# DeltaNet stage of a two-layer hybrid model: the first gate block computed behind the second convolution block, and the output projection's weight splits spread over the levels of the inverse

## The chip, the core and the metric

The kernel runs on one core of one Trainium2 chip. A core has five engines that run side by side and wait for one another on semaphores: TensorE (PE, matrix multiplication), VectorE (DVE), ScalarE (ACT), GpSimd (POOL) and SyncE (SP, here the queue that loads weights). The metric is the device time of one execution in microseconds.

## The reference, cut to what matters

Two layers over 256 tokens of width 1024: sliding-window attention with a dense feed-forward, then a gated DeltaNet with a mixture of 8 experts. The change touches only the gated DeltaNet:

```python
def gated_deltanet(h, w_in, conv_w, a_log, dt_bias, o_norm, w_o):
    proj = h @ w_in                       # 1024 x (4*1024 + 16)
    qkv, z, b, a = split(proj)            # 3072, 1024, 8, 8 columns
    qkv = silu(causal_depthwise_conv(qkv, conv_w))   # 4 taps
    q, k, v = heads(qkv)                  # 8 heads of 128
    q, k = l2_normalize(q), l2_normalize(k)
    beta = sigmoid(b); g = -exp(a_log) * softplus(a + dt_bias)
    o = chunked_gated_delta_rule(q, k, v, g, beta)   # needs a triangular inverse
    o = rms_norm(o, o_norm) * silu(z)     # z is the gate
    return o @ w_o
```

All of it is computed in float32.

## The kernel before

A float32 product is made of three TensorE products of float32r halves: every weight block of 128 x 2048 numbers is loaded by SP into one of 6 raw slots (`w_raw`), split by ScalarE into a high part (`split_high`, line 278, `w_high`) and by VectorE into a low part (`split_low`, line 282, `w_low`), each with 3 slots, and then used by TensorE (`mm3`, lines 290 to 292). Block n may be split once block n-3 has been used (semaphore `w_used`), TensorE may use it once its low part is there (`lo_done`), and SP may load block n once block n-6 has been split.

Nothing plans the order at run time: each engine has its own program, written out by hand, and goes through it in order. In the DeltaNet stage the input projection is 8 column blocks of 512, two weight blocks ("halves") each, in the order of `GDN_COLS`: six for q, k and v (`conv(c, half)`), which go through the convolution, and two for the gate z (`gate_piece`). They use weight blocks 0 to 15, the output projection blocks 16 to 19.

A convolution block c goes through this chain: `conv` on TensorE; `first_tap` on ScalarE (line 660); `taps`, 12 instructions on VectorE (line 1672) that read the product from PSUM; `silu` on ScalarE (line 667); `tokens` on TensorE (line 1092), which turns it to rows of tokens; for q and k also `squares` (676), `norms` on GpSimd (461 to 465), `normed` on VectorE (1683), `turn_back` on TensorE (1102) and `turned_back` on ScalarE (683). Beside it the decay is made: once `gate_done` is set, TensorE sums the gates (line 1145), ScalarE copies them (`gcum`, 704, `egc`, 705), GpSimd builds a difference (454) and `gate_rows` (1112), `exponent` (1689) and `decay_exp` (688) finish it. `key_key` (1116) and `lower` (1695, 1697) give the matrix that is inverted, `key_query` (1120) the attention within a chunk.

The inverse goes in levels 1 to 5. In each, TensorE runs `step` (1211) for two halves t of the tokens, VectorE subtracts from the identity (1768), TensorE runs `update` (1224, 1233), ScalarE and VectorE copy the results (756, 765, 1772), and GpSimd masks the matrix for the next level (`masked`, 487) and does a multiplication of its own (500, 502, 504, then 508 with the gate). Pieces of the gate's second block fill TensorE up to level 2. Behind level 2 ScalarE takes the second block of z (`gate_silu(1)`, 744) and splits blocks 16, 17 and 18; VectorE splits 16 and 17 there and 18 behind level 3.

After the inverse come the scan over the two chunks, the output projection, and the experts, which take most of the time.

Of the kernel before, what the change touches and what calls it, by code (L numbers as in the profile page):

```python
# [73 lines left out]
def hybrid_kernel(nc, x, a_norm, a_w_qkv, a_b_qkv, a_sinks, a_w_o, f_norm, f_w_gate, f_w_up, f_w_down,  # L74
# [14 lines left out]
    with ExitStack() as ctx:  # L89
# [130 lines left out]
        GDN_COLS = (2, 3, 0, 1, 4, 5, 6, 7)  # L220
# [308 lines left out]
        def _(act):  # L529
# [111 lines left out]
            def deltanet(n0):  # L641
# [13 lines left out]
                def first_tap(c):  # L655
                    act.wait_ge(w_used, n0 + 2 * c + 2)
                    cb = GDN_COLS[c]
                    for f in range(4):
                        w = 32 + 24 * (TAPS - 1) + 4 * cb + f
                        last = nc.scalar.activation(cv[:, 4 * cb + f, :], PS[:, 2 * (c % 2) + f // 2, T * (f % 2):T * (f % 2) + T],  # L660
                                                    ACT.Copy, scale=cols[:, w:w + 1])
                    last.then_inc(sem("tap0_done"), 1)

                def silu(c):
                    act.wait_ge(sem("taps_done"), c + 1)
                    cb = GDN_COLS[c]
# [22 lines left out]

                split_high(act, n0 + 3)  # L690
# [17 lines left out]
                silu(1)  # L708
                split_high(act, n0 + 8)
                first_tap(2)  # L710
# [4 lines left out]
                split_high(act, n0 + 9)  # L715
                silu(2)
                split_high(act, n0 + 10)
# [4 lines left out]
                split_high(act, n0 + 11)  # L722
                silu(3)
                split_high(act, n0 + 12)
# [16 lines left out]
                def gate_silu(c):  # L741
                    act.wait_ge(w_used, n0 + 14 + 2 * c)
                    for t in range(TT):
                        nc.scalar.activation(z[:, t, c * CH:(c + 1) * CH], PS[:, Z + t, :], ACT.Silu).then_inc(sem("z_done"), 1)
# [160 lines left out]
        def _(pe):  # L905
# [154 lines left out]
            def deltanet(n0):  # L1060
# [3 lines left out]
                def conv(c, half):  # L1064
                    n = n0 + 2 * c + half
                    pe.wait_ge(lo_done, n + 1)
                    if c >= 2 and half == 0:
                        pe.wait_ge(sem("taps_done"), c - 1)
                    wh, wl = high_low(n, 4)
                    for f in range(4):  # L1070
                        for kk in range(4):
# [4 lines left out]
                            last = mm3(PS[:, 2 * (c % 2) + f // 2, T * (f % 2):T * (f % 2) + T], wh[:, kk, col], wl[:, kk, col],  # L1076
# [3 lines left out]
                def tokens(c):  # L1080
                    cb = GDN_COLS[c]
# [6 lines left out]
                    elif c == 5:  # L1088
                        pe.wait_ge(sem("taps_done"), 6)
# [32 lines left out]
                def gate_piece(c, half, t, k0, k1):  # L1122
                    n = n0 + 12 + 2 * c + half
# [18 lines left out]
                conv(1, 1)  # L1142
                pe.wait_ge(sem("gate_done"), 1)
# [32 lines left out]
                pe.wait_ge(sem("taps_done"), 5)  # L1176
                for half in range(2):
                    for t in range(TT):
                        gate_piece(0, half, t, 0, 4)
# [57 lines left out]
                pe.wait_ge(sem("z_done"), 2)  # L1237
# [220 lines left out]
        def _(dve):  # L1458
# [197 lines left out]
            def deltanet(n0):  # L1656
# [7 lines left out]
                def taps(c):  # L1664
                    dve.wait_ge(sem("tap0_done"), c + 1)
                    cb = GDN_COLS[c]
                    for j in range(1, TAPS):
                        for f in range(4):
# [3 lines left out]
                            last = V.scalar_tensor_tensor(out=o, in0=PS[:, 2 * (c % 2) + f // 2, at:at + T - j], scalar=cols[:, w:w + 1],  # L1672
# [51 lines left out]
                split_low(dve, n0 + 7)  # L1724
                exponent(0, B)
                split_low(dve, n0 + 8)
# [6 lines left out]
                split_low(dve, n0 + 9)  # L1733
                split_low(dve, n0 + 10)
                taps(3)
                normed(2)
                split_low(dve, n0 + 11)
                split_low(dve, n0 + 12)
# [25 lines left out]
                for l in range(1, LEVELS):  # L1764
# [8 lines left out]
                    if l == 2:  # L1773
# [270 lines left out]
```

## Time and profile before

| | |
|---|---|
| median of 3 runs | 1637.07 us (1633.76 to 1637.22) |
| the profiled execution's own time | 1634.98 us |
| its span in the profile | 1633.4 us |
| mean granted clock of TensorE | 0.959 of full speed |
| TensorE busy | 1530.7 us (94%) |
| VectorE, ScalarE, GpSimd busy | 1214.0, 993.9, 94.0 us |
| weight loads of this stage | 16 of `in_b_w_in`, 1 MB each, 5.4 us to land |

Read the span first, then the shares. TensorE is busy nearly all the time, but this is an average: the experts' part (from about 663 us) is dense, and the DeltaNet stage (about 387 to 630 us) has waits. What a change of order there is worth is therefore read in the timeline of that stage: which wait of TensorE ends last at which place. "Idle before <- releaser" at the end of a row tells how long the engine had nothing to do before the row's first instruction, and who let it go. Starts and ends of TensorE instructions overlap by a tenth or two of a microsecond, since they are pipelined.

### The profile page before, as it was taken

The page shows a single profiled execution, that of the slowest core. Times are in us where ns is not written, and L with a number is a line of the kernel's source. Part 1 is how long each engine was busy: PE and PEld are TensorE (multiplying, and loading weights), DVE is VectorE, ACT ScalarE, POOL GpSimd, SP SyncE. Part 2 cuts the span into 40 slices and gives each one's busy share as a digit, 9 for nine tenths or more (in the row PEclk, how much of TensorE's full clock was granted, in tenths as well). Part 3 has the DMA queues.
Part 4 walks back from the last instruction along what each step waited for, and adds up shares of the span by engine and source line. Part 5 has one row for each costly group of instructions (what it writes and reads, how often), then busy time and mean ns, then how long its engine had stood idle before and what let it go on. Part 6 is the DMA issues. An engine that isn't in the chain of part 4 may idle for free.

```text
span 1633.4 us, 22310 instructions
## 1 busy us (share of the span) xinstructions
PE 1530.7 (94%) x8225; PEld 1292.4 (79%) x8225; DVE 1214.0 (74%) x983; ACT 993.9 (61%) x931; POOL 94.0 (6%) x104
## 2 busy tenths in 40 slices
PE   5888999998989777899999999999999999999996
PEld 4777888877988676788888888888888888888884
DVE  5744555555576535788888888888888889888887
ACT  4444343434673434577777777777777777777773
POOL 0002000000122401100000000000000000000200
PEclk9789999998899878899999999999999999999998
DMA  9217755553332203699999999999999999999992
GB/s 341 92 39 272 285 187 181 193 191 105 104 129 79 80 1 104 244 377 376 389 380 364 398 375 374 392 377 375 390 367 383 382 381 376 383 380 360 417 409 86
DMA packets 92603, 453.96 MB, mean 278 GB/s; under 512 B 9872, under 2 KB 10256, under 8 KB 49552
## 3 DMA queue, kind: packets, MB, share of 16 engines
q1 hardware_dynamic: 83680, 430.83, 70.0%
q0 software_dynamic: 5616, 20.45, 3.1%
q10 hardware_dynamic: 3264, 2.08, 0.5%
q8 instruction: 31, 0.51, 0.1%
q14 instruction: 12, 0.10, 0.0%
HBM read 437.60 MB, written 15.73 MB: 278 GB/s over the span
## 4 chain that ended last, share of the span: by engine, by line
PE 90%; ACT 4%; DVE 4%; issue 1%; ACTq 1%; POOL 0%; DVEq 0%; POOLq 0%
PE PS L290 27%; PE PS L292 27%; PE PS L291 27%; PE PS L1348 1%; PE PS L917 1%; ACT w_high L278 1%; DVE w_low L282 1%; PE PS L991 1%; PE PS L1233 1%; ACT xs L562 1%; PE PS L967 1%; PE PS L1280 0%; PE PS L1224 0%; PE PS L980 0%; ACTq L549 0%
## 5 line engine op out<-in xcount | busy, mean ns | idle before, releaser
L282 DVE TENSOR_TENSOR w_low<-w_raw,w_high 128x2048 fp32r<-128x2048 f32 x408 | 936.1, 2297 | 238.5 <-ACT w_high L278 238.0
L278 ACT ACTIVATE w_high<-w_raw 128x2048 fp32r<-128x2048 f32 x408 | 781.3, 1918 | 361.1 <-PE PS L292 359.0
L290 PE MATMUL PS<-w_high,x_high 128*128 128x512 f32 x1264 | 501.5, 397 | 5.9 <-DVE x_low L1866 4.5
L292 PE MATMUL PS<-w_high,x_low 128*128 128x512 f32 x1264 | 494.1, 391 | 0.0
L291 PE MATMUL PS<-w_low,x_high 128*128 128x512 f32 x1264 | 493.6, 391 | 0.0
L290 PEld LDWEIGHTS PS<-w_high,x_high 128*128 128x128 f32 x1264 | 238.4, 189 | 56.1 <-DVE x_low L1866 4.6
L292 PEld LDWEIGHTS PS<-w_high,x_low 128*128 128x128 f32 x1264 | 238.1, 188 | 50.8
L291 PEld LDWEIGHTS PS<-w_low,x_high 128*128 128x128 f32 x1264 | 238.5, 189 | 47.4
L290 PE MATMUL PS<-w_high,m_act_high 128*128 128x512 f32 x448 | 175.0, 391 | 1.6 <-DVE m_act_low L1929 1.6
L292 PE MATMUL PS<-w_high,m_act_low 128*128 128x512 f32 x448 | 174.4, 389 | 0.0
L291 PE MATMUL PS<-w_low,m_act_high 128*128 128x512 f32 x448 | 174.4, 389 | 0.0
L290 PEld LDWEIGHTS PS<-w_high,m_act_high 128*128 128x128 f32 x448 | 84.1, 188 | 19.0 <-DVE m_act_low L1929 1.8
L292 PEld LDWEIGHTS PS<-w_high,m_act_low 128*128 128x128 f32 x448 | 84.1, 188 | 17.5
L291 PEld LDWEIGHTS PS<-w_low,m_act_high 128*128 128x128 f32 x448 | 84.1, 188 | 17.2
L833 ACT ACTIVATE m_act_high<-PS 128x512 fp32r<-128x512 f32 x56 | 33.6, 600 | 70.1 <-PE PS L1348 70.1
L290 PE MATMUL PS<-x_high,w_high 128*128 128x256 f32 x192 | 57.2, 298 | 0.0
L291 PE MATMUL PS<-x_low,w_high 128*128 128x256 f32 x192 | 56.1, 292 | 0.0
L292 PE MATMUL PS<-x_high,w_low 128*128 128x256 f32 x192 | 56.0, 292 | 0.0
L917 PE MATMUL PS<-cst,xs 128*128 128x128 f32 x96 | 21.9, 422 | 32.6 <-DVE xs L1481 25.2
L917 PEld LDWEIGHTS PS<-cst,xs 128*128 128x128 f32 x96 | 19.6, 225 | 34.5 <-DVE xs L1481 26.7
L1495 DVE TENSOR_TENSOR h<-PS,h 128x512 f32<-128x512 f32 x36 | 22.6, 685 | 30.4 <-PE PS L292 30.4
L290 PE MATMUL PS<-w_high,f_act_high 128*128 128x512 f32 x112 | 44.4, 397 | 0.7 <-DVE f_act_low L1623 0.7
(272 smaller groups left out, 1282.8 us busy)
## 6 DMA issues: line engine op xcount, KB each, us to landing
w_raw<-in_m_w_blocks SPq DMA_DIRECT2D x336, 1024.0 KB, 7.0
w_raw<-in_b_w_in SPq DMA_DIRECT2D x16, 1024.0 KB, 5.4
w_raw<-in_f_w_gate SPq DMA_DIRECT2D x14, 1024.0 KB, 5.0
w_raw<-in_f_w_up SPq DMA_DIRECT2D x14, 1024.0 KB, 5.0
w_raw<-in_f_w_down SPq DMA_DIRECT2D x14, 1024.0 KB, 4.8
w_raw<-in_a_w_qkv SPq DMA_DIRECT2D x6, 1024.0 KB, 13.1
x_slots_dram<-zeros POOLq DMA_DIRECT2D x12, 512.0 KB, 7.5
w_raw<-in_a_w_o SPq DMA_DIRECT2D x4, 1024.0 KB, 6.9
```

What stands on the lines that cost most here:

```text
L278: nc.scalar.activation(WH[:, n % SPLIT, :], W[:, n % RAW, :], ACT.Copy).then_inc(hi_done, 1)
L282: nc.vector.tensor_tensor(WL[:, n % SPLIT, :], W[:, n % RAW, :], WH[:, n % SPLIT, :].bitcast(f32), ALU.subtract).then_inc(lo_done, 1)
L290: nc.tensor.matmul(o, sH, mH, start=first, stop=False)
L291: nc.tensor.matmul(o, sH, mL, start=False, stop=False)
L292: return nc.tensor.matmul(o, sL, mH, start=False, stop=last)
L562: nc.scalar.activation(xs[:, t], h[:, t], ACT.Square, accum_out=ss[:, n, t:t + 1]).then_inc(ss_done, 1)
L833: nc.scalar.activation(maH[:], PS[:, 4, :].rearrange("p (f q) -> p f q", f=4), ACT.Copy)\
L917: last = nc.tensor.transpose(PS[:, 4 + b, 256 * kk + 128 * t:256 * kk + 128 * t + 128], src[:, t, 128 * k:128 * k + 128], ident)
L967: last = nc.tensor.matmul(PS[:, 2 * (a % 2) + hh % 2, col:col + nk], qkT[r, hd // 2, 128 * t:128 * t + 128], qkT[r, 8 + g, 0:nk], start=Tr ...
L991: last = nc.tensor.matmul(PS[:, 6 + a % 2, 64 * hh:64 * hh + 64], probT[:, a % 2, hh * (t + 1) + kt, :], qkv[:, kt, 1280 + 64 * g:1280 + 6 ...
L1233: last = nc.tensor.matmul(PS[halves(s), A + s, HALF * hh:HALF * hh + HALF], Zt[halves(s), t, hh, :], X[halves(s), t, hh, :], start=True, s ...
L1495: return V.tensor_tensor(h[:, t, cb * CH:(cb + 1) * CH], PS[:, bank, :], h[:, t, cb * CH:(cb + 1) * CH], ALU.add)
```

## The change

The weight blocks are taken in another order: the gate's first column block (6) becomes the third of the eight. TensorE computes it (48 products of 512 columns) directly behind `conv(1)`, ahead of the wait for `gate_done`, where it used to run behind `key_key(1)`, after the last convolution block. ScalarE's `gate_silu(0)` moves from behind `silu(5)` to behind `silu(1)`. `CONV_AT` and `GATE_AT` give the place of each block among the eight, `CONV_BANK` the PSUM banks of each convolution block: blocks 2 and 3 change places, so that `conv(2)` waits for `taps(1)` and `conv(3)` for the gate's SiLU. The splits of blocks 4 to 15 move with the blocks. Of the output projection's blocks, 16 is now split behind `v_evict(4)` and `taps(5)`, 17 behind level 1, and 18 behind level 3 on both engines; none behind level 2.

```diff
-        GDN_COLS = (2, 3, 0, 1, 4, 5, 6, 7)
+        GDN_COLS = (2, 3, 6, 0, 1, 4, 5, 7)
+        CONV_AT = (0, 1, 3, 4, 5, 6)
+        GATE_AT = (2, 7)
+        CONV_BANK = (0, 2, 2, 0, 2, 0)
...
                 def first_tap(c):
-                    act.wait_ge(w_used, n0 + 2 * c + 2)
-                    cb = GDN_COLS[c]
+                    act.wait_ge(w_used, n0 + 2 * CONV_AT[c] + 2)
+                    cb = GDN_COLS[CONV_AT[c]]
...
+                def gate_silu(c):
+                    act.wait_ge(w_used, n0 + 2 * GATE_AT[c] + 2)
+                    for t in range(TT):
+                        nc.scalar.activation(z[:, t, c * CH:(c + 1) * CH], PS[:, Z + t, :], ACT.Silu).then_inc(sem("z_done"), 1)
...
                 squares(0)
                 split_high(act, n0 + 7)
                 silu(1)
+                gate_silu(0)
                 split_high(act, n0 + 8)
+                split_high(act, n0 + 9)
+                split_high(act, n0 + 10)
                 first_tap(2)
...
-                split_high(act, n0 + 13)
+                split_high(act, n0 + 15)
                 silu(4)
-                split_high(act, n0 + 14)
                 first_tap(5)
...
                 v_evict(4)
-                split_high(act, n0 + 15)
+                split_high(act, n0 + 16)
                 silu(5)
-                gate_silu(0)
                 turned_back(3)
                 v_evict(5)
...
+                    if l == 1:
+                        split_high(act, n0 + 17)
                     if l == 2:
                         gate_silu(1)
-                        split_high(act, n0 + 16)
-                        split_high(act, n0 + 17)
+                    if l == 3:
                         split_high(act, n0 + 18)
...
                 def conv(c, half):
-                    n = n0 + 2 * c + half
+                    n = n0 + 2 * CONV_AT[c] + half
                     pe.wait_ge(lo_done, n + 1)
-                    if c >= 2 and half == 0:
-                        pe.wait_ge(sem("taps_done"), c - 1)
+                    if half == 0 and c == 3:
+                        pe.wait_ge(sem("z_done"), 2)
+                    elif half == 0 and c >= 2:
+                        pe.wait_ge(sem("taps_done"), (2, 0, 3, 4)[c - 2])
...
                 conv(1, 0)
                 conv(1, 1)
+                pe.wait_ge(sem("taps_done"), 1)
+                for half in range(2):
+                    for t in range(TT):
+                        gate_piece(0, half, t, 0, 4)
                 pe.wait_ge(sem("gate_done"), 1)
...
                 key_key(1)
-                pe.wait_ge(sem("taps_done"), 5)
-                for half in range(2):
-                    for t in range(TT):
-                        gate_piece(0, half, t, 0, 4)
                 pe.wait_ge(sem("u_read"), 2)
                 turn_back(3)
                 tokens(5)
...
-                pe.wait_ge(sem("z_done"), 2)
+                pe.wait_ge(sem("taps_done"), 6)
                 gate_piece(1, 0, 0, 0, 4)
...
                 normed(0)
                 split_low(dve, n0 + 7)
+                split_low(dve, n0 + 8)
                 exponent(0, B)
-                split_low(dve, n0 + 8)
+                split_low(dve, n0 + 9)
+                split_low(dve, n0 + 10)
                 taps(2)
...
-                split_low(dve, n0 + 13)
+                split_low(dve, n0 + 15)
                 lower(0)
-                split_low(dve, n0 + 14)
                 lower(1)
                 taps(5)
-                split_low(dve, n0 + 15)
+                split_low(dve, n0 + 16)
...
-                    if l == 2:
-                        split_low(dve, n0 + 16)
+                    if l == 1:
                         split_low(dve, n0 + 17)
                     if l == 3:
                         split_low(dve, n0 + 18)
```

What is left out: the definitions of `silu`, `taps` and `tokens`, which take their column block and banks from the new tables, `gate_silu`'s old place, the numbers of the splits between `taps(2)` and `taps(4)` (each higher by 2), and `tokens(5)`, which waits for `taps(4)` instead of `taps(5)`.

TensorE's order behind `conv(1)`, before: the last products of `conv(1)` (128x256), the sums of the gates (gate,cst), `tokens(0)` (cst,cv), then `conv(2)`.

```order
L290 MATMUL PS<-x_high,w_high 128x256
L291 MATMUL PS<-x_low,w_high 128x256
L292 MATMUL PS<-x_high,w_low 128x256
L1145 MATMUL PS<-gate,cst 128x16 x2
L1092 MATMUL PS<-cst,cv 128x128 x8
L290 MATMUL PS<-x_high,w_high 128x256
```

The same place after the change: the last products of the gate block (128x512), the sums, `tokens(0)`, `conv(2)`.

```order
L293 MATMUL PS<-w_high,x_high 128x512
L294 MATMUL PS<-w_low,x_high 128x512
L295 MATMUL PS<-w_high,x_low 128x512
L1156 MATMUL PS<-gate,cst 128x16 x2
L1099 MATMUL PS<-cst,cv 128x128 x8
L293 MATMUL PS<-x_high,w_high 128x256
```

The sums of the gates now stand behind the 48 products of the gate block instead of directly behind `conv(1)`.

VectorE's order in the inverse, before, from the first level: `step` is the subtraction, invT the copy of a level's result, w_low a split.

```order
L1768 TENSOR_TENSOR step<-cst,PS 64x512 x4
L1772 COPY invT<-PS 64x512 x2
L1768 TENSOR_TENSOR step<-cst,PS 64x512 x4
L1772 COPY invT<-PS 64x512 x2
L282 TENSOR_TENSOR w_low<-w_raw,w_high 128x2048 x2
L1768 TENSOR_TENSOR step<-cst,PS 64x512 x4
L1772 COPY invT<-PS 64x512 x2
L282 TENSOR_TENSOR w_low<-w_raw,w_high 128x2048
L1768 TENSOR_TENSOR step<-cst,PS 64x512 x4
```

The same place after the change.

```order
L1776 TENSOR_TENSOR step<-cst,PS 64x512 x4
L1780 COPY invT<-PS 64x512 x2
L285 TENSOR_TENSOR w_low<-w_raw,w_high 128x2048
L1776 TENSOR_TENSOR step<-cst,PS 64x512 x4
L1780 COPY invT<-PS 64x512 x2
L1776 TENSOR_TENSOR step<-cst,PS 64x512 x4
L1780 COPY invT<-PS 64x512 x2
L285 TENSOR_TENSOR w_low<-w_raw,w_high 128x2048
L1776 TENSOR_TENSOR step<-cst,PS 64x512 x4
```

The two splits between levels 2 and 3 are gone; one stands between levels 1 and 2, the other of them ahead of the inverse.

## Rows read from the trace of the kernel before

**Rows 1.** The timeline, TensorE behind conv(1): start us, us, engine line op

```profile
425.15 0.62 PE L1145 MATMUL PS<-gate,cst 128*128 128x16 f32 x4 [1.64 <-DVE beta L1716]
426.86 1.81 PE L1092 MATMUL PS<-cst,cv 128*128 128x128 f32 x8 [1.09 <-ACT cv L667]
437.81 0.36 PE L290 MATMUL PS<-x_high,w_high 128*128 128x256 f32 x1
443.65 1.03 PE L1092 MATMUL PS<-cst,cv 128*128 128x128 f32 x8
```

**Rows 2.** The timeline, ScalarE, GpSimd and VectorE ahead of the second half of conv(2)

```profile
429.94 0.20 ACT L704 ACTIVATE gcum<-PS 128x16 f32<-128x16 f32 x1
431.70 3.75 POOL L454 TENSOR_TENSOR decay<-cst,gcum 128x1024 f32<-128x1024 f32 x2 [4.52 <-ACT egc L705]
437.60 1.29 DVE L1683 TENSOR_TENSOR tok<-PS,rq 128x512 f32<-128x512 f32 x2 [1.65 <-POOL rq L462]
438.81 2.28 DVE L282 TENSOR_TENSOR w_low<-w_raw,w_high 128x2048 fp32r<-128x2048 f32 x1
```

**Rows 3.** The timeline, TensorE, from the end of conv(5) to the gate's second block

```profile
493.92 1.03 PE L1092 MATMUL PS<-cst,cv 128*128 128x128 f32 x8
496.50 0.47 PE L290 MATMUL PS<-w_high,x_high 128*128 128x512 f32 x1
507.49 1.03 PE L1102 MATMUL PS<-cst,tok 128*128 128x128 f32 x8
509.75 3.84 PE L1120 MATMUL PS<-cv 128*128 128x128 f32 x32 [0.34 <-ACT cv L683]
513.34 0.47 PE L290 MATMUL PS<-w_high,x_high 128*128 128x512 f32 x1
```

**Rows 4.** The timeline, VectorE and ScalarE, the last convolution block

```profile
498.33 1.38 DVE L1695 TENSOR_TENSOR u_diag<-PS,decay 64x512 f32<-64x512 f32 x2
500.36 5.00 DVE L1672 SCALAR_TENSOR_TENSOR cv<-PS,cols,cv 128x255 f32<-128x255 f32 x12
505.39 1.06 ACT L667 ACTIVATE cv<-cv 128x1024 f32<-128x1024 f32 x1 [1.17 <-DVE cv L1672]
```

**Rows 5.** The timeline, TensorE, levels 2 to 4 of the inverse

```profile
531.41 2.03 PE L1211 MATMUL PS<-invT,u_level 64*64 64x64 f32 x64
536.34 1.15 PE L1224 MATMUL PS<-step,inv 64*64 64x64 f32 x32
540.70 2.03 PE L1211 MATMUL PS<-invT,u_level 64*64 64x64 f32 x64
552.06 1.97 PE L1224 MATMUL PS<-step,inv 64*64 64x64 f32 x32 [9.33 <-DVE step L1768]
558.01 2.03 PE L1211 MATMUL PS<-invT,u_level 64*64 64x64 f32 x64
561.73 1.15 PE L1224 MATMUL PS<-step,inv 64*64 64x64 f32 x32 [0.67 <-DVE step L1768]
```

**Rows 6.** The timeline, ScalarE and VectorE behind level 2 of the inverse

```profile
542.13 1.08 ACT L744 ACTIVATE xs<-PS 128x512 f32<-128x512 f32 x2
543.10 5.51 ACT L278 ACTIVATE w_high<-w_raw 128x2048 fp32r<-128x2048 f32 x3
550.62 2.80 DVE L1768 TENSOR_TENSOR step<-cst,PS 64x512 f32<-64x512 f32 x4
```

**Rows 7.** The timeline, GpSimd beside the levels, and the VectorE split at its third row

```profile
535.10 1.89 POOL L502 TENSOR_TENSOR tok<-tok,egc 128x1024 f32<-128x1024 f32 x1
559.20 2.20 POOL L487 TENSOR_TENSOR u_level<-u_diag,cst 128x512 f32<-128x512 f32 x1 [12.96 <-PE PS L1211]
557.97 2.29 DVE L282 TENSOR_TENSOR w_low<-w_raw,w_high 128x2048 fp32r<-128x2048 f32 x1
```

**Rows 8.** The windows: TensorE's granted clock is the third number from the right

```profile
425.00:430.00 5.00, 3.75 (x20) 3.66 (x21) 1.46 (x2) 4.99 (x8) 2.02 (x2) 0.71 0.37 142
```

**Rows 9.** The timeline, TensorE behind a longer wait, at tokens(3)

```profile
478.12 1.85 PE L1102 MATMUL PS<-cst,tok 128*128 128x128 f32 x8 [3.56 <-ACT cv L683]
```

More of the change, by code:

```diff
@@ L655, in first_tap @@
                 def first_tap(c):
[L656 to L657 removed]
+                    act.wait_ge(w_used, n0 + 2 * CONV_AT[c] + 2)
+                    cb = GDN_COLS[CONV_AT[c]]
                     for f in range(4):
                         w = 32 + 24 * (TAPS - 1) + 4 * cb + f
[L660 removed]
+                        last = nc.scalar.activation(cv[:, 4 * cb + f, :], PS[:, CONV_BANK[c] + f // 2, T * (f % 2):T * (f % 2) + T],
                                                     ACT.Copy, scale=cols[:, w:w + 1])
@@ L714, in deltanet @@
                 squares(1)
-                split_high(act, n0 + 9)
+                split_high(act, n0 + 11)
                 silu(2)
-                split_high(act, n0 + 10)
+                split_high(act, n0 + 12)
                 first_tap(3)
@@ L1075, in conv @@
                             col = slice(128 * f, 128 * f + 128)
-                            last = mm3(PS[:, 2 * (c % 2) + f // 2, T * (f % 2):T * (f % 2) + T], wh[:, kk, col], wl[:, kk, col],
+                            last = mm3(PS[:, CONV_BANK[c] + f // 2, T * (f % 2):T * (f % 2) + T], wh[:, kk, col], wl[:, kk, col],
                                        xH[:, k, :], xL[:, k, :], k == 0 and f % 2 == 0, k == KD - 1 and f % 2 == 1)
@@ L1122, in gate_piece @@
                 def gate_piece(c, half, t, k0, k1):
-                    n = n0 + 12 + 2 * c + half
+                    n = n0 + 2 * GATE_AT[c] + half
                     pe.wait_ge(lo_done, n + 1)
@@ L1175, in deltanet @@
                 key_key(1)
-                pe.wait_ge(sem("taps_done"), 5)
-                for half in range(2):
-                    for t in range(TT):
-                        gate_piece(0, half, t, 0, 4)
                 pe.wait_ge(sem("u_read"), 2)
@@ L1671, in taps @@
                             at = T * (f % 2)
-                            last = V.scalar_tensor_tensor(out=o, in0=PS[:, 2 * (c % 2) + f // 2, at:at + T - j], scalar=cols[:, w:w + 1],
+                            last = V.scalar_tensor_tensor(out=o, in0=PS[:, CONV_BANK[c] + f // 2, at:at + T - j], scalar=cols[:, w:w + 1],
                                                           in1=o, op0=ALU.mult, op1=ALU.add)
@@ L1732, in deltanet @@
                 normed(1)
-                split_low(dve, n0 + 9)
-                split_low(dve, n0 + 10)
+                split_low(dve, n0 + 11)
+                split_low(dve, n0 + 12)
                 taps(3)
                 normed(2)
-                split_low(dve, n0 + 11)
-                split_low(dve, n0 + 12)
+                split_low(dve, n0 + 13)
+                split_low(dve, n0 + 14)
                 taps(4)
                 normed(3)
-                split_low(dve, n0 + 13)
+                split_low(dve, n0 + 15)
                 lower(0)
-                split_low(dve, n0 + 14)
                 lower(1)
                 taps(5)
-                split_low(dve, n0 + 15)
+                split_low(dve, n0 + 16)
                 for t in range(TT):
```

15 lines of the change are left out of this document (6 added, 9 removed).

## The prediction

> **What bounds the kernel now.** I read the page first: TensorE is busy 94% of the span. Then I read the windows over the DeltaNet stage, to see where it is not, and then the timeline of TensorE there, and at each of its waits the timeline of the engine that ends it. Three places matter, since the change touches them.
>
> Behind `conv(1)` TensorE waits 1.64 us for the gates and, after a few tiny products, 1.09 us for `silu(0)` [rows 1]. The clock granted in that stretch is 0.71 on average [rows 8], so for part of it the engine ran at 1.2 instead of 2.4 GHz; eight transposes take 1.81 us where they take 1.03 us later [rows 1]. So this is a real hole, a few microseconds deep.
>
> From the end of `conv(5)` on TensorE has hardly a wait: `tokens(4)` and `key_key(1)` from 493.92 to 496.50, the gate block to 507.49, then `turn_back(3)` and `tokens(5)`, and `key_query` from 509.75 to 513.34 [rows 3]. In that time VectorE and ScalarE finish the last convolution block [rows 4]. The gate block (10.99 us) is their cover.
>
> In the inverse TensorE stands still for 9.33 us behind level 2 [rows 5], since ScalarE first does the gate's SiLU and three splits (5.51 us) and VectorE two splits before its subtractions [rows 6].
>
> **The change, part by part.** The work itself is unchanged in number and size: the same 48 products, the same splits, the same SiLU. No load is larger, and blocks are requested when an older one has been split, two places ahead as before. I give the loads nothing: the blocks that the change hurries (4 to 7) were asked for long before. What changes is who waits where.
>
> *Front.* TensorE leaves `conv(1)` at about 423.4 (the row at 425.15 less its wait, and a little overlap) and goes on with the gate block, 10.99 us, to 434.35. Its two weight blocks are split by then. The sums of the gates follow, 0.62 us [rows 1], done at 434.97. Only now may ScalarE copy them. From that copy to the end of a split on VectorE the chain takes 429.94 to 441.09, that is 11.15 us: copy and table load and exponential on ScalarE, two differences on GpSimd (3.75 us), the norms there, two multiplications on VectorE, the split [rows 2]. Before, that split was for a block needed much later. Now it is `split_low(7)`, and the second half of `conv(2)` needs it. So that half starts at 434.97 + 11.15 + 0.05 = 446.17, where it started at 437.81 [rows 1]: +8.4 us, with a gate block of 10.99 us done in between. The hole is smaller by 2.6 us, and not closed. TensorE reaches this wait at about 443.6, from the end of `taps(1)` at 435.9 with half a block (437.81 to 443.65, 5.84 us) and the 16 `gate_rows` of 1.8 us behind it (an estimate from twice the eight transposes), so it stands for 2.5 us. From there to the end of `conv(5)` every engine does the same as before, 8.4 us later; splits two blocks further on are as far ahead of their use as before.
>
> *Tail.* Behind `key_key(1)` the gate block is gone. `lower(1)` starts when `key_key(1)` is done, 2.58 us after the end of `conv(5)` plus 0.3 for the last product to end. Then come `lower(1)`, 2.03 (498.33 to 500.36), `taps(5)`, 5.03, `silu(5)`, 1.06 [rows 4], `tokens(5)`, 0.9, and `key_query`, 3.59 (509.75 to 513.34) [rows 3]. With 0.05 for the handover that is 2.58 + 0.3 + 2.03 + 5.03 + 1.06 + 0.05 + 0.9 + 3.59 = 15.5 us, against 513.34 - 493.92 = 19.4 us before. So removing 10.99 us of work wins 3.9 us here. TensorE now waits about 2.1 us for `lower(1)` (its u_read) and 5 us for `silu(5)`. `turn_back(3)` between them is off the path.
>
> *Inverse.* Behind level 1 ScalarE has its turn 1.4 us after the next step has started (542.13 less 540.70), splits block 17 in 1.84 us (a third of 5.51), and VectorE splits it in 2.29 us and makes half of its subtractions in 1.4 us [rows 5 to 7]. With handovers, `update` starts 7.05 us after `step`. In level 2 it started 4.93 us after it (531.41 to 536.34), behind a gate piece: +2.1 us. Level 3 loses its wait of 9.33 us: `step` to `update` takes 1.19 (559.20 less 558.01) + 1.40 = 2.6 us instead of 11.36, and `update` to the next `step` 4.36 (536.34 to 540.70) instead of 5.95 [rows 5 to 7]: -10.4 us. In level 4 the split of block 18 by both engines again gives 7.05 us instead of 3.72: +3.3 us. Sum: 2.12 - 10.35 + 3.33 = -4.9 us.
>
> GpSimd makes this worse. At 559.20 its masking of 512 columns took 2.20 us, more than 1024 columns at 535.10 (1.89 us), while VectorE's split ran until 560.26 [rows 7]. So one of these two engines holds the other off. Behind level 1 the split now meets GpSimd's masking and its `egc` multiplication, and behind level 3 the masking and the multiplication by `o_w`, twice 1024 columns. If the split only waits for a masking that has begun, each costs 0.4 us more. If it must also wait for the multiplication, it is 1.9 us and 3.8 us (twice 1.89) more. I take 0.4 at both places and half of 1.9 at the first: +1.8 us. So the inverse wins 3.1 us, with bounds of a gain of 4.9 and a loss of 1.6 us (all three).
>
> The Trainium skill, "GPSIMD Engine Reference", section "Specifications", says that GpSimd shares its SBUF interfaces with VectorE, and that contention is with instructions in a two-port mode or with two SBUF inputs. By it the splits are hit and `taps`, which read PSUM, are not; the row at 559.20 agrees. Without that rule and row the sum would be 1.8 us lower.
>
> *The clock.* After a wait of 3.56 us eight transposes took 1.85 us [rows 9], as after the 1.64 and 1.09 us at the front [rows 1]; in level 3 the slow stretch cost 5.95 - 4.36 = 1.6 us. So I price a fall at 1.6 us. At the tail there are 7 us of waits: 2.0 (1.6 to 3.4). In level 4 the wait is near 5 us: 1.2. The 2.5 us at `conv(2)` and the 2.5 us or more in level 2 may or may not bring a fall: 0.7 and 0.6, each between 0 and 1.6. The fall behind `tokens(3)` may not come again: -0.5 (-1.6 to 0). Sum +4.0 us.
>
> The Trainium skill, "TensorE: Matmul & The Clock Gate", section "Why this matters for your kernels", warns only of idle gaps above about 3 us. By it the two waits of 2.5 us would cost no clock, and the sum would be 1.3 us lower; rows 1, where two shorter waits brought a fall, speak against it.
>
> *Sum.* 8.4 - 3.9 - 3.1 + 4.0 = +5.4 us. Behind the inverse all is as before, and the experts start later by what the stage is longer. The profiled execution took 1634.98 us (span 1633.4), so the sum gives 1640.4. That execution lies 2.1 us below the median of the runs (1637.07) and 1.2 above the fastest; I go about a quarter of the way to the median and forecast 1641.0 us.
>
> **The rivals.** *A tie.* VectorE gets ahead of GpSimd at both places and the two doubtful falls of the clock don't come: 8.4 - 3.9 - 4.1 + 1.6 + 0.5 - 0.5 = +2.0 us, 1637.0 to 1639. For it speaks that VectorE's split at 557.97 was not held off [rows 7]. Against it, GpSimd was the second to come there.
>
> *Faster.* The tail's cover is not needed, and the hole at the front closes. This decides if the chain of `lower(1)`, `taps(5)` and `silu(5)` takes at most 1 us more than TensorE's other work: then the tail wins the whole 10.99 us, and the stage moves by 8.4 - 11 - 4.1 + 1 = -5.7 us, to 1629. If the split of block 7 also came in time, it would be -8, 1627. For it speaks the wait of 9.33 us, which goes for certain. Against it, the rows of the last block add up to 8.1 us without any wait inside, and VectorE can't begin sooner, as its order puts `lower(1)` ahead of `taps(5)`.
>
> *Much slower.* GpSimd's multiplications go first at both places and the clock falls at every wait: 8.4 - 3.9 + 1.6 + 7 = +13, 1648. It needs three coincidences.
>
> *The change does nothing.* The new block is not split in time and TensorE waits at its new place for what it waited for before. The splits of blocks 4 and 5 were not late for `conv(2)` before, so this has little to stand on; 1637.
>
> **How the numbers follow.** Less than 0.2%, 3.3 us, can't be told from no change. The forecast (+3.3 to +9) has 0.50, much slower 0.12, the tie 0.24, nothing 0.05, faster 0.09. So slower 0.62, same 0.29, faster 0.09. The range leaves out most of "faster" and the end of "much slower": 1635.5 to 1647.
>
> **What would show it.** Right: a TensorE wait near 2.5 us ahead of the second half of `conv(2)`, released by VectorE's split; waits near 2 and 5 us between `key_key(1)` and `tokens(5)`; no wait of 9 us in the inverse, but one of 2 to 4 us in level 2 and of 4 us or more in level 4, both released by the subtraction; splits there longer than 2.3 us where GpSimd runs. Wrong: `conv(2)` without a wait, `tokens(5)` within 1 us of `turn_back(3)`, or an experts' part whose length differs from before.

## The result, and the profile after

| | before | after |
|---|---|---|
| median | 1634.38 us (7 runs, 1633.39 to 1640.55) | 1646.54 us (7 runs, 1640.34 to 1649.28) |
| profiled execution: span, mean granted clock | 1633.4 us, 0.959 | 1647.7 us, 0.951 |

The ratio is 1.0064, with a 95% interval of 1.0044 to 1.0084: the change makes the kernel slower, by about 10 us (1634.4 x 0.0064). The two medians are 12.2 us apart; the ratio comes from all the runs. The forecast was 1641.0 us, +5.4. Three of the seven runs lie above 1647, the upper end of the stated range.

The timeline of TensorE behind `conv(1)` in the changed kernel (start us, us, engine, line, operation; the wait before it and its releaser in brackets):

```profile
436.88 0.51 PE L1156 MATMUL PS<-gate,cst 128*128 128x16 f32 x4
448.62 0.38 PE L293 MATMUL PS<-x_high,w_high 128*128 128x256 f32 x1 [2.21 <-DVE w_low L285]
455.96 1.03 PE L1099 MATMUL PS<-cst,cv 128*128 128x128 f32 x8
```

The waits of 1.64 and 1.09 us [rows 1] are gone, and a new one of 2.21 us stands where the prediction put it, released by VectorE's split. The half block behind it takes 7.34 us (448.62 to 455.96) instead of 5.84: the clock fell. The chain that sets it, answering to rows 2, on ScalarE, GpSimd and VectorE:

```profile
437.42 0.18 ACT L712 ACTIVATE gcum<-PS 128x16 f32<-128x16 f32 x1 [4.74 <-PE PS L1156]
...
439.17 3.75 POOL L457 TENSOR_TENSOR decay<-cst,gcum 128x1024 f32<-128x1024 f32 x2 [9.37 <-ACT egc L713]
...
445.08 1.29 DVE L1690 TENSOR_TENSOR tok<-PS,rq 128x512 f32<-128x512 f32 x2 [5.71 <-POOL rq L465]
446.28 4.48 DVE L285 TENSOR_TENSOR w_low<-w_raw,w_high 128x2048 fp32r<-128x2048 f32 x2
```

The first of the two splits in the last row is block 7. From 437.42 to 448.57, its end, are 11.15 us, as before.

The tail, answering to rows 3, on TensorE:

```profile
506.20 1.03 PE L1099 MATMUL PS<-cst,cv 128*128 128x128 f32 x8
507.07 1.95 PE L1123 MATMUL PS<-cv 128*128 128x128 f32 x16
511.29 1.72 PE L1109 MATMUL PS<-cst,tok 128*128 128x128 f32 x8 [2.27 <-DVE u_cross L1704]
517.30 1.97 PE L1099 MATMUL PS<-cst,cv 128*128 128x128 f32 x8 [4.30 <-ACT cv L670]
519.06 5.06 PE L1127 MATMUL PS<-cv 128*128 128x128 f32 x32
523.88 0.47 PE L293 MATMUL PS<-w_high,x_high 128*128 128x512 f32 x1
```

Two waits have taken the gate block's place, 2.27 us for `lower(1)` and 4.30 us for `silu(5)`, and the two groups of eight transposes and `key_query` behind them run partly at the half clock (5.06 instead of 3.84 us).

The inverse, answering to rows 5, on TensorE:

```profile
541.97 2.03 PE L1218 MATMUL PS<-invT,u_level 64*64 64x64 f32 x64
...
549.31 1.97 PE L1231 MATMUL PS<-step,inv 64*64 64x64 f32 x32 [2.33 <-DVE step L1776]
...
555.12 2.03 PE L1218 MATMUL PS<-invT,u_level 64*64 64x64 f32 x64
...
562.07 2.03 PE L1218 MATMUL PS<-invT,u_level 64*64 64x64 f32 x64
...
569.39 1.81 PE L1231 MATMUL PS<-step,inv 64*64 64x64 f32 x32 [4.26 <-DVE step L1776]
```

Level 3 (555.12 to 562.07) takes 6.95 us instead of 17.3; the wait of 9.33 us has become one of 2.33 in level 2 and one of 4.26 in level 4. Beside them, VectorE and GpSimd, answering to rows 7:

```profile
545.35 2.50 DVE L285 TENSOR_TENSOR w_low<-w_raw,w_high 128x2048 fp32r<-128x2048 f32 x1 [3.98 <-ACT w_high L281]
...
565.45 2.47 DVE L285 TENSOR_TENSOR w_low<-w_raw,w_high 128x2048 fp32r<-128x2048 f32 x1 [3.98 <-ACT w_high L281]
```

```profile
545.66 3.94 POOL L505 TENSOR_TENSOR tok<-tok,egc 128x1024 f32<-128x1024 f32 x1
...
565.72 6.58 POOL L511 TENSOR_TENSOR xs<-xs,o_w 128x2048 f32<-128x2048 f32 x1
```

The split loses 0.2 us, and it is GpSimd that is held off: 3.94 instead of 1.89 us. This costs nobody anything.

Behind the inverse the code is the same in both kernels, and yet it is longer. The windows from the first product of the output projection to the experts' first transposes, and from there to the choice of tokens (busy times of PE, PEld, DVE, ACT, POOL; third from the right the granted clock), before:

```profile
607.99:635.25 27.26, 22.05 (x99) 17.93 (x97) 10.30 (x13) 8.79 (x10) 1.98 (x4) 1.00 0.33 106
635.25:651.87 16.62, 13.08 (x74) 12.87 (x75) 11.69 (x30) 8.42 (x12) 4.67 (x2) 0.60 0.22 80
```

and after:

```profile
618.10:646.61 28.51, 23.30 (x99) 18.87 (x97) 10.30 (x13) 8.79 (x10) 1.98 (x4) 0.92 0.30 102
646.61:666.15 19.54, 16.01 (x75) 15.82 (x75) 11.59 (x30) 8.44 (x12) 4.68 (x2) 0.50 0.17 67
```

In the second window the clock is at 1.2 GHz from end to end, where before it was at 2.4 GHz for a part; that is 2.92 us, and 1.25 us in the first. Nothing waits longer for another engine. Below, the *short form* is a profile in which projection and router together take 46.7 to 47.3 us, the *long form* one in which they take 51.0 to 51.4 us; no profile lies between.

This table cuts the profile at fixed places of TensorE's timeline. *Front*: the stage's first transposes to the second half of `conv(2)`; *middle*: to the end of `conv(5)`; *tail*: to the gate's second block; *inverse*: to the last transposes of k and q; *scan*: to the transposes ahead of the projection; *projection*: from those to the experts' first transposes; *router*: from those to the choice. All in us; the runs further down are in it too. The experts take 969.5 to 970.2 us in every one.

| kernel | front | middle | tail | inverse | scan | projection | router |
|---|---|---|---|---|---|---|---|
| before | 50.33 | 56.11 | 19.42 | 62.20 | 29.12 | 30.59 | 16.62 |
| before, 2nd profile | 50.46 | 56.09 | 19.42 | 62.31 | 29.12 | 30.63 | 16.59 |
| after | 58.56 | 57.58 | 17.68 | 60.75 | 30.15 | 31.83 | 19.54 |
| after, 2nd profile | 58.70 | 57.20 | 18.00 | 60.44 | 30.35 | 30.47 | 16.69 |
| after, 3rd profile | 58.51 | 57.56 | 17.70 | 60.70 | 30.15 | 31.86 | 19.56 |
| splits only | 50.34 | 56.12 | 19.45 | 60.57 | 30.62 | 30.60 | 16.55 |
| gate only | 58.61 | 57.13 | 17.96 | 61.85 | 29.10 | 30.35 | 16.77 |
| after, front mended | 56.05 | 56.04 | 17.94 | 60.59 | 30.24 | 30.42 | 16.72 |
| after, tail mended | 58.57 | 57.60 | 15.79 | 59.31 | 30.14 | 31.80 | 19.55 |
| before, splits in the scan | 50.32 | 56.14 | 19.44 | 51.13 | 30.23 | 30.42 | 16.75 |
| after, all three mends | 56.19 | 56.01 | 16.17 | 51.11 | 29.22 | 31.49 | 19.55 |
| splits in the scan, front closed | 44.72 | 57.41 | 19.42 | 51.10 | 29.22 | 31.52 | 19.54 |
| the same, with filler | 44.61 | 57.45 | 19.44 | 51.12 | 30.70 | 29.51 | 17.76 |
| after, with filler | 58.66 | 57.13 | 17.98 | 60.43 | 30.34 | 30.46 | 16.27 |

### The profile page after: what moved, and what is told of

The parts are those of the page before. It is cut to its first block, busy times and chain, and to the rows that moved or that the text cites. A ratio compares the mean times of both kernels' runs of the same rounds, so it can differ in the third digit from the quotient of the medians.

```text
span 1647.7 us, 22310 instructions
## 1 busy us (share of the span) xinstructions
PE 1542.2 (94%) x8225; PEld 1301.9 (79%) x8225; DVE 1213.1 (74%) x983; ACT 994.1 (60%) x931; POOL 97.3 (6%) x104
## 4 chain that ended last, share of the span: by engine, by line
PE 91%; ACT 4%; DVE 3%; POOL 1%; ACTq 1%; issue 1%; POOLq 0%; DVEq 0%
PE PS L293 27%; PE PS L295 27%; PE PS L294 27%; PE PS L1355 1%; PE PS L922 1%; ACT w_high L281 1%; PE PS L996 1%; PE PS L1240 1%; ACT xs L565 1%; PE PS L972 1%; PE PS L985 0%; PE PS L1287 0%; ACTq L552 0%; DVE w_low L285 0%; PE PS L1231 0%
## 5 line engine op out<-in xcount | busy, mean ns | idle before, releaser
L295 PEld LDWEIGHTS PS<-w_high,x_low 128*128 128x128 f32 x1264 | 238.6, 189 | 51.1
```

Source lines behind the costliest of these rows:

```text
L295: return nc.tensor.matmul(o, sL, mH, start=False, stop=last)
```

## The experiments

Theory A: the loss is the sum of the waits and of the clock they bring, as predicted: the gate block had been the cover of the last convolution block. Theory B, formed on the table's last columns: much of it is the clock in code behind the inverse. All timed runs are against the kernel before on the same chip.

**Only the splits moved.** The kernel before, with:

```diff
+                split_high(act, n0 + 16)          # behind v_evict(5)
...
+                    if l == 1:
+                        split_high(act, n0 + 17)
                     if l == 2:
                         gate_silu(1)
-                        split_high(act, n0 + 16)
-                        split_high(act, n0 + 17)
-                        split_high(act, n0 + 18)
+                    if l == 3:
+                        split_high(act, n0 + 18)
```

and the same on VectorE (16 behind the attention products, 17 behind level 1; 18 stays behind level 3).

> The kernel before, with only the output projection's splits moved: block 16 behind the last copies ahead of the inverse, 17 behind level 1, 18 behind level 3 on both engines. The gate block stays where it was. By the theory of the waits, the inverse alone wins what it won in the changed kernel: level 3 about -10.4 us, level 2 about +2.4 and level 4 about +3.6 us of wait, and up to two falls of the clock at 1.45 us each: -1.5 to -4.5 us against the kernel before. The rival, that the splits inside the levels cost as much as they save, expects a tie or slower.

Measured: 1634.27 against 1634.49 us, ratio 0.9997 (0.9988 to 1.0007). A tie; the expected gain of 1.5 us is just inside the interval, 4.5 are not. On TensorE the profile has three waits for the subtractions instead of the one of 9.33 us:

```profile
539.44 1.22 PE L1226 MATMUL PS<-step,inv 64*64 64x64 f32 x32 [2.33 <-DVE step L1771]
547.35 1.15 PE L1226 MATMUL PS<-step,inv 64*64 64x64 f32 x32 [0.55 <-DVE step L1771]
559.03 1.97 PE L1226 MATMUL PS<-step,inv 64*64 64x64 f32 x32 [4.26 <-DVE step L1771]
```

In the table the inverse wins 1.6 us and the scan gives back 1.5 at a granted clock of 0.72 instead of 0.76. So the forecast for the inverse alone was met at its lower end, that for the kernel was not: here this half of the change is worth nothing.

**Only the gate block moved.** The changed kernel with the splits of 16, 17 and 18 back behind level 2 (18's low part behind level 3):

```diff
-                split_high(act, n0 + 16)          # behind v_evict(4), ahead of silu(5)
...
-                    if l == 1:
-                        split_high(act, n0 + 17)
                     if l == 2:
                         gate_silu(1)
+                        split_high(act, n0 + 16)
+                        split_high(act, n0 + 17)
+                        split_high(act, n0 + 18)
-                    if l == 3:
-                        split_high(act, n0 + 18)
```

> The changed kernel with the output projection's splits of blocks 16 and 17 put back behind level 2 (and 18's high part with them): only the gate block is moved. By the theory of the waits this part loses 8.2 us at the front and 1.5 us to the clock in conv(2), wins 1.7 us at the tail, and the inverse is as before: about +8 us against the kernel before. The rival, that most of the loss is the clock in the stages behind the inverse, expects +3 us or less here if the phase of those stages is not hit, and the same +10 as the changed kernel if any shift brings it.

Measured: 1643.11 us, ratio 1.0051 (1.0033 to 1.0070), or +8.3 us, as theory A had it. Its profile shows the short form behind the inverse (30.35 and 16.77 us), and is still 9.7 us longer than before: front +8.3, middle +1.0, tail -1.5, the later stretches -0.5 together, and 2.5 us of it ahead of the stage, in code that is the same. The rival that expected 3 us or less is out; the same +10 as the changed kernel lies within the interval (+5.4 to +11.4), but not by way of the long form, which this profile doesn't have. The loss up to the end of the inverse comes with the gate block's move.

**The front mended.** The changed kernel with:

```diff
                 first_tap(1)
+                split_high(act, n0 + 7)
                 act.wait_ge(sem("gcum_ps"), 1)
...
                 squares(0)
-                split_high(act, n0 + 7)
...
                 taps(1)
+                split_low(dve, n0 + 7)
...
                 normed(0)
-                split_low(dve, n0 + 7)
```

> The changed kernel with the split of block 7 moved ahead of the decay chain on ScalarE and VectorE (behind first_tap(1) and taps(1)). By the theory of the waits TensorE's wait of 2.2 us at the second half of conv(2) goes, and with it the fall of the clock of 1.5 us: -2.5 to -4 us against the changed kernel. If the wait there is not on this split, nothing changes.

Measured: 1637.87 us, ratio 1.0021 (1.0007 to 1.0034), against 1.0064 for the changed kernel. The wait is gone; TensorE goes from `gate_rows` straight on:

```profile
443.02 1.95 PE L1119 MATMUL PS<-cst,gate_wide 128*128 128x128 f32 x16
```

```profile
444.72 0.36 PE L293 MATMUL PS<-x_high,w_high 128*128 128x256 f32 x1
```

In the table front and middle are 4.0 us shorter than in the first profile after (2.5 and 1.5). That is the forecast's upper end. The ratios differ by more, 0.0043 or about 7 us. In the two profiles the rest is in projection and router, which are in the short form here (by 4.2 us); against the second profile after, which has the short form too, front and middle are 3.8 us shorter. What made up the 7 us in the other runs no profile shows.

**The tail mended.** The changed kernel with:

```diff
-                lower(1)
                 taps(5)
+                lower(1)
```

> The changed kernel with taps(5) ahead of lower(1) on VectorE. taps(5) can start when first_tap(5) is done, 3.2 us earlier; turn_back(3) then waits for lower(1) behind it. By the theory of the waits key_query starts about 2 us earlier than in the changed kernel: -1 to -2.5 us. If the tail is not bound by this chain of VectorE, no change.

Measured: 1644.10 us, ratio 1.0046 (1.0027 to 1.0065). The interval overlaps that of the changed kernel, so the time alone doesn't settle it; the table has the tail 1.9 us shorter, as expected (and the inverse 1.4, which was not), with one wait of 6.07 us in place of two:

```profile
513.86 1.97 PE L1109 MATMUL PS<-cst,tok 128*128 128x128 f32 x8 [6.07 <-DVE u_cross L1704]
```

**The splits in the scan.** The kernel before, with block 16 split ahead of the inverse and:

```diff
+                split_high(act, n0 + 17)          # ahead of the levels
...
+                split_high(act, n0 + 18)          # behind the copies "tg"
...
                         last.then_inc(sem("zt_done"), 1)
+                    if l == 1:
+                        split_low(dve, n0 + 17)
...
+                split_low(dve, n0 + 18)           # behind the cross terms
```

and no split behind levels 2 and 3. Of the three blocks only VectorE's split of 17 is still inside the levels, behind the subtractions of level 1.

> The kernel before, with the output projection's splits where both engines wait anyway: block 16 ahead of the inverse, 17 on ScalarE ahead of level 1 and on VectorE behind the subtractions of level 1, 18 in the scan (behind the copies tg on ScalarE and behind the cross terms on VectorE). By the theory of the waits the three levels have none of the splits' waits: level 3 -10.4 us, level 4 -0.5, and nothing is given back: -9 to -11 us less what the clock takes in the scan (1 to 1.5): about -9 us against the kernel before. The rival, that the clock gives back whatever the inverse wins (as it did when the splits were only spread), expects -3 us or less.

Measured: 1626.13 us against 1635.19, ratio 0.9952 (0.9939 to 0.9965): -7.8 us (the medians are 9.1 apart). The expected 9 are within the interval, the rival's 3 are not. On TensorE level 3 is 6.94 us (541.47 to 548.41) and level 4 has no wait behind the transposes at 550.38:

```profile
541.47 2.03 PE L1211 MATMUL PS<-invT,u_level 64*64 64x64 f32 x64
544.05 1.15 PE L1224 MATMUL PS<-step,inv 64*64 64x64 f32 x32 [0.55 <-DVE step L1769]
...
548.41 2.03 PE L1211 MATMUL PS<-invT,u_level 64*64 64x64 f32 x64
550.38 1.09 PE L1250 MATMUL PS<-cst,tok 128*128 128x128 f32 x8
551.40 1.15 PE L1224 MATMUL PS<-step,inv 64*64 64x64 f32 x32
```

**The changed kernel with all three mends.**

> The changed kernel with three mends at once: block 7's split ahead of the decay chain, taps(5) ahead of lower(1), and the output projection's splits placed as in the run with the splits in the scan. If the place of the gate block costs only what its two new waits cost, this is within 2 us of the kernel before with those splits. If the cover at the tail is worth more than the hole at the front, as the sum of the waits has it (front mended -10.99 + 5.7 + hole, tail 7 us of waits less 2), it is 1 to 4 us slower than that kernel.

Measured: 1628.28 us, ratio 0.9963 (0.9951 to 0.9975). The median is 2.2 us above the unmoved kernel with the same splits (1626.13), but the intervals overlap (0.9939 to 0.9965 there), and its profile has the long form behind the inverse. Up to the end of the inverse the table has 179.5 us against 177.0, so 2.5 us for the move; the scan, with the same code, is 1.0 us shorter. The moved block is then no gain; that it is a loss rests on the profiles, not on the times, and neither of the two expectations (within 2 us, or 1 to 4 us slower) is ruled out.

**The front closed without moving the gate block.** The kernel with the splits in the scan, and on ScalarE:

```diff
                 first_tap(0)
-                split_high(act, n0 + 5)
                 act.wait_ge(sem("gate_in"), 1)
...
                 silu(0)
+                split_high(act, n0 + 5)
                 split_high(act, n0 + 6)
```

on VectorE the same for the gates and `split_low` of block 5, and the difference `kdec` ahead of `taps(1)`.

> The kernel before with the splits in the scan, and the hole at the front closed without moving the gate block: ScalarE makes the gates' exponentials and silu(0) ahead of the split of block 5, while it waits for TensorE, VectorE the same, and the decay's difference ahead of taps(1). By the theory of the waits TensorE no longer waits behind conv(1), and the second half of conv(2) starts 4 to 5.4 us earlier: -4 to -5.5 us against the kernel with the splits in the scan. The rival, that another wait (the decay chain ahead of gate_rows) takes the place, expects -1 us or less.

Measured: 1622.52 us, ratio 0.9925 (0.9912 to 0.9937), or 3.6 us less between the medians than with the splits in the scan alone (1626.13 on the same chip; the intervals don't overlap), and 4.4 by the ratios, where 4 to 5.5 were expected. The front is 5.6 us shorter; the middle, 1.3 us longer, takes part of it back. The profiled execution is the slowest of the five (1628.81; the others 1620.89 to 1623.79): it has the long form, and it enters the stage at 392.85 where the kernel with the splits in the scan does at 388.18. TensorE has no wait left behind `conv(1)`:

```profile
428.84 0.52 PE L1145 MATMUL PS<-gate,cst 128*128 128x16 f32 x4
429.21 1.07 PE L1092 MATMUL PS<-cst,cv 128*128 128x128 f32 x8
```

**Idle products in a wait.** The changed kernel with:

```diff
+                for _ in range(40):
+                    nc.tensor.matmul(PS[:, 7, 0:T], xH[:, 0, 0:128], xH[:, 1, :], start=True, stop=True)
                 turn("moe", xs, xs_done, 2 * (norm_no["moe"] + 1))
```

> The changed kernel with 40 more products of 256 columns on TensorE, whose results nothing reads, directly behind the output projection, in its wait of 5.2 us for the experts' norm. It tests the clock: in the changed kernel's profile the half clock lasts from the projection through the router. If the 2.9 us that the router takes longer there are the clock that the wait brings, the router's stretch is as short as before or shorter (16.6 us or less from its transposes to the choice) and the kernel 1 to 3 us faster than the changed one. If the clock falls there for other reasons, the time is the same within 1 us or longer.

Measured: 1644.38 us, ratio 1.0059 (1.0045 to 1.0073), not to be told from the changed kernel; the gain of 1 to 3 us that was expected if the wait makes the form is not seen. Its router takes 16.27 us, but its projection, ahead of the filler, is already in the short form. So this run doesn't settle what makes the form.

**The changed kernel again**, unaltered, twice, and the kernel before once.

> The changed kernel once more, unaltered, for its spread and a second profile. The profiles so far fall in two groups in the code that the change doesn't touch: projection and router take 47.1 to 47.4 us or 51.0 to 51.4 us. If that is chance of the clock and not of the change, this has both groups in its times, a lower end near 1640 and an upper near 1649, and the ratio is again between 1.004 and 1.008. If the changed kernel is always in the long group, none of its profiles shows the short one.

> The changed kernel, unaltered, for a third profile. From its first transposes to the end of the inverse 194.6 us as in the first, within the clock's falls (1.5 us each); projection and router in either group.

> The kernel before, unaltered, for a second profile. By chance of the clock it may show the long group in projection and router (51 us); if the group belongs to the change, it shows the short one (47.2 us) again. Either way the stage up to the end of the inverse takes 188.1 us from its first transposes.

Measured: 1643.57 us (1640.34 to 1648.18), ratio 1.0062 (1.0045 to 1.0080); the third time, a single run, 1647.43; the kernel before, a single run, 1636.40. Up to the end of the inverse the third profile after has 194.5 us and the second before 188.3, as expected (194.6 and 188.1). The third after has the long form, the second before the short one. The windows of the second profile after, for the same two stretches:

```profile
615.77:643.03 27.26, 22.05 (x99) 17.92 (x98) 10.33 (x13) 8.87 (x11) 1.99 (x4) 1.00 0.32 105
643.03:659.72 16.69, 13.15 (x75) 12.93 (x75) 11.76 (x30) 8.35 (x12) 4.68 (x2) 0.60 0.24 81
```

So the same program takes these 4.1 us in one execution and not in another. The long form doesn't belong to the change alone: three other kernels show it as well. But the times of the changed kernel spread over 9 us (1640.3 to 1649.3 in 14 runs), and those of the kernel before mostly over 5 (1631.5 to 1636.5 in 26 runs; the highest of all is 1640.55). The one profile of the change in the short form has a span 7.4 us above the first of before (1640.8 against 1633.4), those in the long form 12.4 and 14.3 us.

The mean granted clock of each execution is on record too. The changed kernel's seven slowest runs (1646.5 to 1649.3 us) are at 0.951 to 0.953, where its two profiles in the long form are; its other seven (1640.3 to 1645.6) are at 0.955 to 0.961, with the one in the short form. Of the kernel before none of the 48 runs beside the experiments is below 0.959, and its two profiles, both in the short form, are at 0.959 and 0.961. This speaks for the long form being more frequent with the change. It doesn't show it, since the mean is that of the whole execution.

**With idle products in the best kernel.** The kernel with the front closed, with 45 such products ahead of the projection's transposes and 40 ahead of the experts'.

> The kernel before with the splits in the scan and the front closed, and with idle products on TensorE in the two waits ahead of the projection's and the experts' transposes (45 and 40 of 256 columns, results unread). If the clock that these waits bring is what makes projection and router long or short, both are in the short group, and the time is 1 to 4 us below the same kernel without them (1622.5), with less spread. The rival expects no change, or up to 1 us more where a filler ends behind what it waits for.

Measured: 1620.61 us (4 runs, 1618.74 to 1620.92), ratio 0.9912 (0.9898 to 0.9927). It is the fastest of all, about 14 us below the kernel before. Its median is 1.9 us below the same kernel without the filler, as expected, but the intervals overlap (0.9912 to 0.9937 there), and the two ran on different chips. In the profile projection and router take 47.3 us instead of 51.1, and the scan, which holds the first filler, 1.5 us more. The windows:

```profile
592.71:619.93 27.22, 26.79 (x137) 22.84 (x137) 10.50 (x14) 8.66 (x10) 1.99 (x4) 1.00 0.32 109
619.93:637.69 17.76, 13.09 (x74) 12.65 (x74) 13.31 (x30) 8.12 (x12) 6.72 (x2) 0.63 0.19 71
```

But the profile without the filler was the slowest of its five runs, and one profile in the short form may be chance. A gain of the filler is not shown.

## Why the prediction was right, and where its size was off

**The direction and the mechanism.** With the clock's falls put where they were expected, the sum has four parts. *Front* +8.4 us: measured +8.2 (58.56 - 50.33), with the wait released as said, and gone when the split was put elsewhere. *Tail* -3.9 and +2.0 for the clock, -1.9: measured -1.7, and two waits of 2.27 and 4.30 us where 2.1 and 5 were forecast. *Inverse* -3.1 and +1.8 for the clock, -1.3: measured -1.5. *Clock in conv(2)* and behind the wait of 3.56 us of rows 9 (it is at `turn_back(2)`, behind `tokens(3)`), +0.7 and -0.5: measured +1.5, as the first fall came in full and the second again. Up to the end of the inverse this is +6.5 us against a sum of +5.4.

**Two terms that were mis-sized, with a sum that came out by luck.** In the inverse I charged 1.8 us for the interface that VectorE and GpSimd share. The splits took 0.2 us longer each; GpSimd carried the rest, off the path. Without the clock the levels so won 4.3 us, where 3.1 were forecast. What made up for it was the clock, 1.45 us in each of the two levels (the level from 549.31 to 555.12 takes 5.81 us, and 4.36 undisturbed) where I had taken 1.2 and 0.6.

**The step that failed** is "Behind the inverse all is as before". The code is, the clock is not: the scan takes 1.0 us more, and projection and router 4.2 us more in the profiled execution. Of the 14.3 us between the spans, 6.5 are the terms of the sum, 5.2 this, and 2.6 were there before the stage began (390.06 against 387.48), in code that is the same. These 2.6 us are chance: the other two profiles after begin the stage at 387.87 and 388.63, the second before at 388.71. The second profile after, without the long form, is at +7.4 us: 6.3 up to the end of the inverse, 1.2 in the scan. So about 7.5 us of the loss are in a profile of either form, and the long form adds 4.1 to 4.3 where it comes. By the granted clocks above it came in about half of the runs, and that would put the median at 1646.5 rather than 1641; this last step is argued, not shown. The forecast also had some luck with its base: it started from 1634.98 and a median of 1637.07 in three runs, and the kernel before has a median of 1634.38 in seven. So a change of 10 to 12 us, twice the one in the sum, came out only 5.5 us above the forecast, and 0.5 us inside the range.

**The rivals.** "Faster" fell on its own condition: the last block's chain is 6.6 us longer than TensorE's other work (the two waits together), not 1. Of what "A tie" needed, VectorE did get ahead of GpSimd at both places, but the two doubtful falls of the clock came in full. "Does nothing" is out, since the waits moved as the order said. "Much slower" rested on GpSimd going first, which it did not; its 1648 was reached in three of the seven runs all the same, and the profiled one of these got there by another road, the clock behind the inverse.

What stays open: what decides between the short and the long form of projection and router, and whether the change makes the long one more frequent, for which the granted clocks speak, or the executions only fell so. The long form is not bound to the moved gate block: the kernel with the front closed, which leaves the block in its place, has it too.

## What to carry to other kernels

Before moving a block of work out of a place, ask what runs on the other engines beside it: 11 us of products that covered a chain of 8 us on VectorE and ScalarE were worth only 1.7 us when they left, the clock's fall included. Closing a hole with work from elsewhere also pushes back what stood behind the hole, here the first link of a chain of 11 us that fed the next weights; it was cheaper to start the late chain earlier, by putting it ahead of a split that waits for TensorE anyway (-5.6 us at the front, -3.6 between the medians). And work that is needed only some 60 us later should leave the waits of a latency-bound loop: spread over the levels the splits won nothing; ahead of the inverse, behind a level's subtractions and in the scan they won 7.8 us.

## What the runs showed of the hardware

- Of two elementwise instructions with both inputs in SBUF, one on VectorE and one on GpSimd, the later waited for nearly all of the earlier here. Above, the split runs from 545.35 to 547.85; the multiplication on GpSimd, begun at 545.66, ends at 549.60. Had it stood still to 547.85 and then taken its 1.89 us, it would end at 549.74. The other way round, in the kernel before behind `conv(2)`, on VectorE and on GpSimd:

```profile
469.54 2.89 DVE L282 TENSOR_TENSOR w_low<-w_raw,w_high 128x2048 fp32r<-128x2048 f32 x1
```

```profile
468.38 1.90 POOL L470 TENSOR_TENSOR decay<-decay,beta 128x1024 f32<-128x1024 f32 x1
```

  GpSimd ends at 470.28; the split would end at 470.28 + 2.29 = 472.57 and ends at 472.43. The Trainium skill ("SBUF — State Buffer", section "SBUF: two separate sides") says that of a VectorE instruction with two SBUF inputs and a GpSimd instruction that reads SBUF, whichever starts first has the shared pair of ports for the whole instruction, and the other fully blocks. Both pairs here agree with this within 0.14 us. The split that came first took 2.50 us all the same, where 2.29 is usual.
- A wait that is cut in two can cost more clock than one long wait. One wait of 9.33 us brought the half clock once in the inverse (5.95 instead of 4.36 us); waits of 2.33 and 4.26 us brought it twice (5.81 and 5.78 us).
- Behind a wait of 2.21 us the clock fell to 1.2 GHz for a time (48 products took 7.34 instead of 5.84 us); behind one of 1.38 us, at 479.17 in the changed kernel, it did not. The length of the wait doesn't decide alone: behind the same wait of 2.3 us at the end of the inverse the eight transposes took 1.09 us in the kernel before (575.54) and 1.97 in the changed one (584.63).
- The same program shows the router at a granted clock of 0.60 in one execution and 0.50 in the next, 16.7 or 19.6 us, without any difference in waits.
